# Gate rows gathered as high and low parts, overflow tables one chunk later, squares added in pairs on GpSimd, in a float32 decoder trunk

## The chip, the cores and the metric

One core of a Trainium2 chip runs the whole program. The metric is the device time of one execution in microseconds, the median over several runs. PE is the matmul engine (TensorE), DVE is VectorE, ACT ScalarE, POOL GpSimd, SP the engine that issues most transfers.

## The reference, cut to what matters

256 tokens of 1024 channels pass two layers of a token mixer and a channel mixer, all in float32.

```python
for layer in range(2):
    h = rms_norm(x, mix_norm[layer])
    x = x + hybrid_mixer(h, ...)
    h = rms_norm(x, ffn_norm[layer])
    x = x + (swiglu(h, ...) if layer == 0 else moe_ffn(h, ...))
return rms_norm(x, final_norm)

# in hybrid_mixer
a, b, p, gc, gp = split(h @ w_in)
u = a * sigmoid(b)
u = depthwise_conv(u, 31 taps, 512 channels) + bias     # causal
u = silu(layer_norm(u))                                  # over the 512 channels
merged = sigmoid(gc) * (u @ w_conv_out) + sigmoid(gp) * pooled(p) * pool_scale
return merged @ w_out

# in moe_ffn: 8 experts, each token goes to its best 2
y = sum_e comb[:, e] * (silu(t @ w_gate[e]) * (t @ w_up[e])) @ w_down[e]
```

## The kernel before, in words

Weights are streamed from HBM in units of 128 x 2048 numbers (1 MB), by SP, into a ring of places. For each unit ACT writes the high part (`w_hi`, line 674, a rounding to the one-pass matmul format) and DVE the low part (`w_lo`, line 1008, the difference). A product is then three one-pass matmuls, high by high, high by low, low by high (lines 1482 to 1484). A unit's place among the split places comes free when PE has used the unit (`unit_used`). Units are numbered within a mixer as U+0, U+1, ..., and within an item (one expert with the up to 128 tokens that go to it) from U0; "unit 11" of an item is U0+11. PE takes them in this order, and ACT and DVE go through them in it too, with their other work placed between splits by hand: `split_to(n)` brings an engine's splits up to unit n-1. The order of each engine's instructions is what the program text says; nothing is planned at run time.

**Mixer.** Each layer's mixer goes through 21 units. u is made by ACT (sigmoid, line 766) and DVE (`u_rows`, line 1125) in two halves, turned by PE (line 1561), copied by ACT. The convolution is 4 blocks of channels (c = 0 to 3) by 31 taps of 128x256: DVE does c = 0, c = 2 and the last taps of c = 3 (line 1057, with sums in PSUM); the other taps are products by ACT (line 709), added up by POOL (line 595). `SHARED` says how many taps of c = 3 go that way. DVE joins the two sums of c = 3 (line 1068). In the midst of slab U+12 PE runs `statistics` between the slab's two units: four plain float32 matmuls for the mean (line 1618), the matmuls of the pooling windows (lines 1572 to 1574), four for the variance (line 1624). A plain float32 matmul appears as two passes. Between mean and variance DVE subtracts the mean (line 1163), and ACT squares (line 815) into `sq`, half of the channels at a time. DVE goes on with splits up to U+15 behind the subtraction.

**Router and first item.** After the second mixer PE computes logits, ranks and totals; DVE makes tables of which token goes to which row of which item. An expert with more than 128 tokens gets an extra item; `overflow_tables` and `combination_table` serve those. The first item is started early: its gate products are computed for all 256 tokens at once (`gate_of_all_tokens`, units 0 and 1), and the rows of its tokens are then picked by a matmul with the 0/1 matrix `onehot`, in `gather_gate` (line 1814), which runs between units 2 and 3. Its source `gate_rows` is ACT's copy of the two PSUM banks (line 933). The token columns are picked in `gather_turned`; ACT and DVE split them (lines 904 and 1378).

**Items.** Items 0 to 7 have 7 chunks (c = 0 to 6) of 6 units each. In a chunk DVE multiplies silu of gate by up (line 1427), PE turns the result (line 1662) between the chunk's first and second gate units, ACT and DVE split it (lines 928 and 1402). In item 0's chunk c = 1 the gate units are 4 and 5, and the product of that chunk is followed by the tables and then by the splits of units 11 and 12. An item's result is added to `sums` in HBM by an indirect transfer in the item after it.

**End.** All but the last item's share is read back from `sums` into `xs` (line 491), the final norm of it made by ACT and DVE (from line 972 and line 1450), and rows of the last item are treated apart.

```python
            sp.wait_ge(scattered, n_items * 16)
            for b in range(TB):
                sp.dma_start(xs[:, b, :], sums[b * P:(b + 1) * P, :]).then_inc(sums_landed, 16)
```

Of the kernel before, what the change touches and what calls it, by code (L numbers as in the profile page):

```python
# [45 lines left out]
def trunk_kernel(nc, x, mix_norm, w_in, conv_dw, conv_dw_b, conv_ln_g, conv_ln_b, w_conv_out, w_pool, pool_scale,  # L46
# [19 lines left out]
    SHARED = 13  # L66
# [157 lines left out]
    with ExitStack() as ctx:  # L224
# [91 lines left out]
        gate_rows = tok_rows  # L316
# [45 lines left out]
        mean_done, centred, centred_sq, var_done = sem("mean_done"), sem("centred"), sem("centred_sq"), sem("var_done")  # L362
        std_ready, normed, silu_conv = sem("std_ready"), sem("normed"), sem("silu_conv")
# [6 lines left out]
        gate_copied, gate_gathered = sem("gate_copied"), sem("gate_gathered")  # L370
# [62 lines left out]
        def _(sp):  # L433
# [55 lines left out]
            sp.wait_ge(scattered, n_items * 16)  # L489
            for b in range(TB):  # L490
                sp.dma_start(xs[:, b, :], sums[b * P:(b + 1) * P, :]).then_inc(sums_landed, 16)
# [34 lines left out]
        def _(pool):  # L526
# [61 lines left out]
            for l in range(L):  # L588
# [8 lines left out]

                pool.wait_ge(gain_landed, seen.next(gain_landed, 16))
# [22 lines left out]
            def item(i):  # L621
# [23 lines left out]
                                    bounds_check=S - 1, oob_is_err=False).then_inc(last_base_landed, 16)  # L645
            seen.item = None
# [11 lines left out]
        def _(act):  # L658
# [18 lines left out]
            def rstd(b):  # L677

                return small[:, 6 + b:7 + b]
# [77 lines left out]
            def mixer(l, U, M):  # L757
# [51 lines left out]
                tap_products(l, 44)  # L809
# [122 lines left out]
            for b in range(TB):  # L932
                act.activation(gate_rows[:, b * N:(b + 1) * N], bank[R_LOW[b]][:, :], ACT.Copy, scale=rstd(b)).then_inc(gate_copied, 1)
# [55 lines left out]
        def _(dve):  # L989
# [123 lines left out]
            def mixer(l, U, M, x_left=None, x_right=None):  # L1113
# [27 lines left out]
                conv_taps(8)  # L1141
                split_to(U + 6)
                u_rows(1, M.high)
# [207 lines left out]
            def overflow_tables():  # L1351

                dve.wait_ge(total_done, 1)
                step(dve.tensor_scalar(over[:, 0, :], bank[TOTAL][:, 0:E], float(P), None, ALU.is_gt))
# [18 lines left out]
            overflow_tables()  # L1373
# [33 lines left out]
            def item(i):  # L1407
# [5 lines left out]
                for c in range(FC):  # L1413
# [14 lines left out]
                    if first and c == 1:  # L1428
                        combination_table()
                        dve.wait_ge(tables_ready, 1)  # L1430
                        shares(1, step).then_inc(onehot_ready, 1)
# [45 lines left out]
        def _(pe):  # L1477
# [120 lines left out]
            def mixer(l, U, M, x_right, next_left):  # L1598
# [13 lines left out]
                def statistics():  # L1612
                    for c in range(CC):
                        if c == 1:
                            pe.wait_ge(prod_added, len(ADDS) * l + last_add[c])
                        else:
                            pe.wait_ge(conv_step, CONV_STEPS * l + {0: TAPS + 1, 2: CONV_STEPS - 1, 3: CONV_STEPS}[c])
                        last = nc.tensor.matmul(bank[M.mean][:, 0:S], mean_w[:, :], conv[:, c, :], start=c == 0, stop=c == CC - 1)  # L1618
                    last.then_inc(mean_done, 1)
                    pool_windows(M.pooled)  # L1620
                    for c in range(CC):
                        if c % 2 == 0:
                            pe.wait_ge(centred_sq, seen.next(centred_sq))
                        last = nc.tensor.matmul(bank[M.var][:, 0:S], mean_w[:, :], sq[:, c * S:(c + 1) * S], start=c == 0, stop=c == CC - 1)  # L1624
                    last.then_inc(var_done, 1)
# [184 lines left out]
            def gather_gate():  # L1810

                for h in range(2):
                    for b in range(TB):
                        last = nc.tensor.matmul(low[0][:, h * S:(h + 1) * S], onehot[:, b, :].bitcast(F32),
                                                gate_rows[:, b * N + h * S:b * N + (h + 1) * S], start=b == 0, stop=b == TB - 1)
                last.then_inc(gate_gathered, 1)
# [18 lines left out]
            pe.wait_ge(gate_copied, TB)  # L1835
# [69 lines left out]
```

## Time and profile before

| what | us |
|---|---|
| median of 3 runs (1419.68 to 1420.81) | 1419.75 |
| the profiled execution's own time | 1420.94 |
| its span, first to last instruction | 1419.2 |
| PE busy in the span | 1405.4 |
| DVE busy | 1176.6 |
| ACT busy | 985.3 |
| POOL busy | 212.8 |
| last weight load issued (SP) | 1373.5 |
| last matmul ends | 1409.4 |
| first work on the rows read back from `sums` | 1403.7 |

The mean granted PE clock is 0.997 of full speed. The profiled execution is 1.2 us above the median; what is worked out from its rows is a difference, to be put on either. Times of day in the text (84.22, 489.07) are us from the start of the span.

### The profile page before, as it was taken

The page shows a single profiled execution, that of the slowest core. Times are in us where ns is not written, and L with a number is a line of the kernel's source. Part 1 is how long each engine was busy: PE and PEld are TensorE (multiplying, and loading weights), DVE is VectorE, ACT ScalarE, POOL GpSimd, SP SyncE. Part 2 cuts the span into 40 slices and gives each one's busy share as a digit, 9 for nine tenths or more (in the row PEclk, how much of TensorE's full clock was granted, in tenths as well). Part 3 has the DMA queues.
Part 4 walks back from the last instruction along what each step waited for, and adds up shares of the span by engine and source line. Part 5 has one row for each costly group of instructions (what it writes and reads, how often), then busy time and mean ns, then how long its engine had stood idle before and what let it go on. Part 6 is the DMA issues. An engine that isn't in the chain of part 4 may idle for free.

```text
span 1419.2 us, 18324 instructions
## 1 busy us (share of the span) xinstructions
PE 1405.4 (99%) x6490; PEld 1166.0 (82%) x6490; DVE 1176.6 (83%) x1069; ACT 985.3 (69%) x869; POOL 212.8 (15%) x251
## 2 busy tenths in 40 slices
PE   9999999999999999999999999999999999999997
PEld 7888888888888888888888888888888888888885
DVE  6997544548987998889899898888989889888896
ACT  7765434347765877867867777786786777778675
POOL 6840000005831101001001001000100100100020
PEclk9999999999999999999999999999999999999998
DMA  9656555545548899999999999999999999999992
GB/s 360 213 177 216 181 180 193 191 152 204 171 170 303 287 402 363 370 369 410 375 383 371 390 369 371 388 384 356 409 373 383 370 390 370 368 396 389 363 389 85
DMA packets 197840, 446.45 MB, mean 315 GB/s; under 512 B 8570, under 2 KB 20138, under 8 KB 197792
## 3 DMA queue, kind: packets, MB, share of 16 engines
q1 hardware_dynamic: 192496, 432.57, 80.8%
q0 software_dynamic: 2592, 8.87, 2.3%
q10 hardware_dynamic: 2704, 4.38, 0.9%
q8 instruction: 28, 0.46, 0.1%
q14 instruction: 20, 0.16, 0.0%
HBM read 438.49 MB, written 7.86 MB: 315 GB/s over the span
## 4 chain that ended last, share of the span: by engine, by line
PE 93%; DVE 4%; DMA 1%; ACT 1%; SPq 0%; issue 0%; POOL 0%; ACTq 0%; POOLq 0%
PE bank L1482 29%; PE bank L1484 29%; PE bank L1483 29%; PE bank L1662 2%; DVE bank L1057 2%; DVE w_lo L1008 2%; DMA raw<-in_w_in_dram 1%; PE bank L1540 1%; ACT w_hi L674 1%; PE bank L1829 0%; DMA out_dram<-tokA 0%; SPq L460 0%; PE bank L1624 0%; PE bank L1804 0%; PE bank L1618 0%
## 5 line engine op out<-in xcount | busy, mean ns | idle before, releaser
L1008 DVE TENSOR_TENSOR w_lo<-raw,w_hi 128x2048 fp32r<-128x2048 f32 x256 | 582.8, 2291 | 134.3 <-ACT w_hi L674 134.1
L674 ACT ACTIVATE w_hi<-raw 128x2048 fp32r<-128x2048 f32 x256 | 488.1, 1912 | 200.1 <-PE bank L1484 198.8
L1482 PE MATMUL bank<-w_hi,dT_hi 128*128 128x512 f32 (+1 forms) x756 | 296.3, 392 | 0.0
L1484 PE MATMUL bank<-w_hi,dT_lo 128*128 128x512 f32 (+1 forms) x756 | 293.2, 388 | 0.0
L1483 PE MATMUL bank<-w_lo,dT_hi 128*128 128x512 f32 (+1 forms) x756 | 292.6, 387 | 0.0
L1482 PE MATMUL bank<-w_hi,cT_hi 128*128 128x512 f32 x492 | 194.3, 395 | 0.0
L1484 PE MATMUL bank<-w_hi,cT_lo 128*128 128x512 f32 x492 | 191.7, 390 | 0.0
L1483 PE MATMUL bank<-w_lo,cT_hi 128*128 128x512 f32 x492 | 191.6, 389 | 0.0
L1484 PEld LDWEIGHTS bank<-w_hi,dT_lo 128*128 128x128 f32 x756 | 141.9, 188 | 29.4
L1482 PE MATMUL bank<-w_hi,hT_hi 128*128 128x512 f32 x416 | 164.1, 394 | 1.3 <-DVE hT_lo L1022 1.0
L1482 PEld LDWEIGHTS bank<-w_hi,dT_hi 128*128 128x128 f32 x756 | 142.0, 188 | 28.4
L1483 PEld LDWEIGHTS bank<-w_lo,dT_hi 128*128 128x128 f32 x756 | 142.1, 188 | 28.1
L1484 PE MATMUL bank<-w_hi,hT_lo 128*128 128x512 f32 x416 | 162.1, 390 | 0.0
L1483 PE MATMUL bank<-w_lo,hT_hi 128*128 128x512 f32 x416 | 162.0, 389 | 0.0
L615 POOL TENSOR_TENSOR small<-small 128x1 f32<-128x1 f32 x19 | 31.5, 1657 | 832.5 <-DVE next_rows L1331 458.5
L1008 DVE TENSOR_TENSOR hT_lo<-raw,hT_hi 128x2048 fp32r<-128x2048 f32 x57 | 130.5, 2289 | 10.5 <-ACT hT_hi L674 10.4
L674 ACT ACTIVATE hT_hi<-raw 128x2048 fp32r<-128x2048 f32 x57 | 109.1, 1915 | 20.8 <-PE bank L1484 20.8
L1484 PEld LDWEIGHTS bank<-w_hi,cT_lo 128*128 128x128 f32 x492 | 92.4, 188 | 19.6
L1482 PEld LDWEIGHTS bank<-w_hi,cT_hi 128*128 128x128 f32 x492 | 92.4, 188 | 18.2
L1483 PEld LDWEIGHTS bank<-w_lo,cT_hi 128*128 128x128 f32 x492 | 92.5, 188 | 18.2
L595 POOL TENSOR_TENSOR work<-work,tap_prod 128x256 f32<-128x256 f32 x80 | 91.3, 1142 | 11.8 <-POOL work L595 0.4
L1482 PEld LDWEIGHTS bank<-w_hi,hT_hi 128*128 128x128 f32 x416 | 78.1, 188 | 17.8 <-DVE hT_lo L1022 1.2
(260 smaller groups left out, 1859.0 us busy)
## 6 DMA issues: line engine op xcount, KB each, us to landing
raw<-in_moe_w_gate_dram SPq DMA_DIRECT2D x96, 1024.0 KB, 7.5
raw<-in_moe_w_up_dram SPq DMA_DIRECT2D x72, 1024.0 KB, 10.3
raw<-in_moe_w_down_dram SPq DMA_DIRECT2D x72, 1024.0 KB, 9.0
raw<-in_w_in_dram SPq DMA_DIRECT2D x20, 1024.0 KB, 5.7
mix<-in_moe_w_up_dram SPq DMA_DIRECT2D x16, 1024.0 KB, 8.5
gates<-in_moe_w_down_dram SPq DMA_DIRECT2D x16, 1024.0 KB, 11.2
gates<-in_moe_w_up_dram SPq DMA_DIRECT2D x16, 1024.0 KB, 8.7
work<-in_moe_w_down_dram SPq DMA_DIRECT2D x16, 1024.0 KB, 10.9
```

The lines of the kernel that those rows point to most:

```text
L595: pool.tensor_tensor(conv[:, c, :], part, tap_prod[:, (len(PRODUCTS) * l + n) % PRODS, :], ALU.add).then_inc(prod_added, 1)
L615: pool.tensor_tensor(small[:, 15:16], small[:, 14:15], small[:, 14:15], ALU.add).then_inc(gate_passed, 1)
L674: act.activation(w_hi[split_place(u, seen.item is not None)][:, 0:width], place[slot][:, 0:width], ACT.Copy).then_inc(hi_ready, 1)
L1008: dve.tensor_tensor(w_lo[split][:, 0:width], place[slot][:, 0:width], w_hi[split][:, 0:width].bitcast(F32), ALU.subtract).then_inc(lo_read ...
L1057: ins = dve.scalar_tensor_tensor(dst, src, tap, sum_, ALU.mult, ALU.add)
L1482: nc.tensor.matmul(dst, a_hi, b_hi, start=start, stop=False)
L1483: nc.tensor.matmul(dst, a_hi, b_lo, start=False, stop=False)
L1484: return nc.tensor.matmul(dst, a_lo, b_hi, start=False, stop=stop)
L1540: last = nc.tensor.transpose(bank[banks[k // 2]][:, (k % 2) * S + b * P:(k % 2) * S + (b + 1) * P], source[:, b, k * P:(k + 1) * P], ident ...
L1662: last = nc.tensor.transpose(bank[banks[b]][:, f * P:(f + 1) * P], tokP[:, b, f * P:(f + 1) * P], ident[:, :])
```

## The change

- `SHARED` goes from 13 to 14: one more tap of c = 3, in each layer, is a product by ACT and an add by POOL, one fewer a tap of DVE.
- In the first layer DVE does twelve taps and u's second half, and only then the split of unit U+5; in the second layer the order stays.
- POOL adds the squares of channel blocks 0 and 1, and of 2 and 3; PE's variance takes two matmuls instead of four. The adds stand ahead of POOL's scaling of the pool gates.
- The first item's gate rows are kept as a high part, written by ACT, and a low part, written by DVE, in the tiles `hT_hi` and `hT_lo`; the gather is four one-pass matmuls of 512 columns instead of four plain float32 ones of 256.
- The overflow tables, but for their first instruction, move from before the first item to its second chunk (c = 1), ahead of the combination table.
- The two transfers that read `sums` back are issued by POOL behind its last indirect read, not by SP behind the last weights.

```diff
-    SHARED = 13
+    SHARED = 14
...
-        gate_rows = tok_rows
+        gate_hi, gate_lo = (t[:, :, :].rearrange("p k s -> p (k s)")[:, 0:TB * N] for t in (hT_hi, hT_lo))
...
-            sp.wait_ge(scattered, n_items * 16)
-            for b in range(TB):
-                sp.dma_start(xs[:, b, :], sums[b * P:(b + 1) * P, :]).then_inc(sums_landed, 16)
...
+                for i in range(2):
+                    pool.wait_ge(centred_sq, seen.next(centred_sq))
+                    pair_of = sq[:, 2 * i * S:(2 * i + 1) * S]
+                    pool.tensor_tensor(pair_of, pair_of, sq[:, (2 * i + 1) * S:(2 * i + 2) * S], ALU.add).then_inc(sq_paired, 1)
+
                 pool.wait_ge(gain_landed, seen.next(gain_landed, 16))
...
                                     bounds_check=S - 1, oob_is_err=False).then_inc(last_base_landed, 16)
+            for b in range(TB):
+                pool.dma_start(xs[:, b, :], sums[b * P:(b + 1) * P, :]).then_inc(sums_landed, 16)
...
-                tap_products(l, 44)
+                tap_products(l, 45)
...
-                act.activation(gate_rows[:, b * N:(b + 1) * N], bank[R_LOW[b]][:, :], ACT.Copy, scale=rstd(b)).then_inc(gate_copied, 1)
+                act.activation(gate_hi[:, b * N:(b + 1) * N], bank[R_LOW[b]][:, :], ACT.Copy, scale=rstd(b)).then_inc(gate_hi_ready, 1)
...
-                conv_taps(8)
-                split_to(U + 6)
-                u_rows(1, M.high)
+                if l:
+                    conv_taps(8)
+                    split_to(U + 6)
+                    u_rows(1, M.high)
+                else:
+                    conv_taps(12)
+                    u_rows(1, M.high)
+                    split_to(U + 6)
...
-            overflow_tables()
+            dve.wait_ge(total_done, 1)
+            step(dve.tensor_scalar(over[:, 0, :], bank[TOTAL][:, 0:E], float(P), None, ALU.is_gt))
+            for b in range(TB):
+                part = slice(b * N, (b + 1) * N)
+                dve.wait_ge(gate_hi_ready, b + 1)
+                dve.scalar_tensor_tensor(gate_lo[:, part], bank[R_LOW[b]][:, :], rstd(b), gate_hi[:, part].bitcast(F32), ALU.mult,
+                                         ALU.subtract).then_inc(gate_lo_ready, 1)
...
                     if first and c == 1:
+                        overflow_tables()
                         combination_table()
...
-                    for c in range(CC):
-                        if c % 2 == 0:
-                            pe.wait_ge(centred_sq, seen.next(centred_sq))
-                        last = nc.tensor.matmul(bank[M.var][:, 0:S], mean_w[:, :], sq[:, c * S:(c + 1) * S], start=c == 0, stop=c == CC - 1)
+                    for c in (0, 2):
+                        pe.wait_ge(sq_paired, seen.next(sq_paired))
+                        last = nc.tensor.matmul(bank[M.var][:, 0:S], mean_w[:, :], sq[:, c * S:(c + 1) * S], start=c == 0, stop=c == 2)
...
-                for h in range(2):
-                    for b in range(TB):
-                        last = nc.tensor.matmul(low[0][:, h * S:(h + 1) * S], onehot[:, b, :].bitcast(F32),
-                                                gate_rows[:, b * N + h * S:b * N + (h + 1) * S], start=b == 0, stop=b == TB - 1)
+                pe.wait_ge(gate_lo_ready, TB)
+                for b in range(TB):
+                    for part in (gate_hi, gate_lo):
+                        last = nc.tensor.matmul(low[0], onehot[:, b, :], part[:, b * N:(b + 1) * N],
+                                                start=b == 0 and part is gate_hi, stop=b == TB - 1 and part is gate_lo)
```

## Rows read from the trace of the kernel before

**Rows 1.** The page: busy time of each engine, share of the span, instructions.
```profile
PE 1405.4 (99%) x6490; PEld 1166.0 (82%) x6490; DVE 1176.6 (83%) x1069; ACT 985.3 (69%) x869; POOL 212.8 (15%) x251
```

**Rows 2.** Who waited for whom, PE: us in total, times, longest; first of five.
```profile
PE bank L1670 <- POOL ident L538: 1.6, 1, 1.6
```

**Rows 3.** The chain of work that ended last: start us, us, what.
```profile
87.98 1.82 PE bank L1624 x8
...
396.98 1.82 PE bank L1624 x8
...
464.81 1.73 PE bank L1814 x8
...
488.79 0.44 PE bank L1662 x4
```

**Rows 4.** Timeline, first layer, second half of u: start us, us, engine, line.
```profile
32.61 2.76 DVE L1008 TENSOR_TENSOR w_lo<-raw,w_hi 128x2048 fp32r<-128x2048 f32 x1 [0.34 <-ACT w_hi L674]
...
33.68 0.81 ACT L766 ACTIVATE tokA<-bank,small 128x256 f32<-128x256 f32 x2
...
36.21 0.66 PE L1561 MATMUL bank<-ident,tokA 128*128 128x128 f32 x4 [0.80 <-DVE tokA L1125]
```

**Rows 5.** Timeline, first layer, mean to variance.
```profile
81.92 0.74 POOL L595 TENSOR_TENSOR work<-work,tap_prod 128x256 f32<-128x256 f32 x1
...
84.22 0.42 DVE L1068 TENSOR_TENSOR work<-bank,work 128x256 f32<-128x256 f32 x1
...
86.16 1.23 ACT L815 ACTIVATE work<-work 128x512 f32<-128x512 f32 x2 [1.00 <-DVE work L1163]
...
86.64 3.42 DVE L1008 TENSOR_TENSOR w_lo<-raw,w_hi 128x1024 fp32r<-128x1024 f32 x2
```

**Rows 6.** Timeline, second layer: the second split, and the variance.
```profile
396.77 2.28 DVE L1008 TENSOR_TENSOR w_lo<-raw,w_hi 128x2048 fp32r<-128x2048 f32 x1
...
396.83 1.97 PE L1624 MATMUL bank<-work,mean_w 128*128 128x256 f32 x8
```

**Rows 7.** POOL against DVE: all tap adds (ns min/median/max), then timeline rows.
```profile
L595 POOL TENSOR_TENSOR work<-work,tap_prod x80: 728/742/2834, 29.8 to 391.3; 128x256 f32<-128x256 f32 x80
...
33.36 2.59 POOL L595 TENSOR_TENSOR work<-work,tap_prod 128x256 f32<-128x256 f32 x1
...
638.79 4.50 DVE L1008 TENSOR_TENSOR w_lo<-raw,w_hi 128x2048 fp32r<-128x2048 f32 x2
...
638.94 2.19 POOL L615 TENSOR_TENSOR small<-small 128x1 f32<-128x1 f32 x1 [56.69 <-DVE next_rows L1331]
```

**Rows 8.** Timeline before the first item: first and last table operation, copies, splits.
```profile
458.06 0.23 DVE L1355 TENSOR_TENSOR tap_prod<-tap_prod 128x64 f32<-128x64 f32 x1
...
459.43 1.27 ACT L933 ACTIVATE gates<-bank,small 128x512 f32<-128x512 f32 x2 [6.39 <-issue]
...
460.61 0.17 DVE L1370 TENSOR_TENSOR slot_of<-tap_prod 128x6 f32<-128x6 f32 x1
...
461.33 2.16 DVE L1378 SCALAR_TENSOR_TENSOR dT_lo<-bank,vecs,dT_hi 128x128 fp32r<-128x128 f32 x8 [0.56 <-ACT dT_hi L904]
...
463.47 2.28 DVE L1008 TENSOR_TENSOR w_lo<-raw,w_hi 128x2048 fp32r<-128x2048 f32 x1
```

**Rows 9.** Timeline, DVE in the first item's second chunk.
```profile
483.94 0.68 DVE L1427 TENSOR_TENSOR tokP<-bank,tokA 128x512 f32<-128x512 f32 x1
...
485.94 4.49 DVE L1008 TENSOR_TENSOR w_lo<-raw,w_hi 128x2048 fp32r<-128x2048 f32 x2
```

**Rows 10.** Before the tail: timeline, DMA to landing, and a window's busy us and clock.
```profile
1359.68 2.73 POOL L644 DMA_INDIRECT gates<-sums,current_row  x1 [0.57 <-issue]
...
1398.10 1.92 ACT L674 ACTIVATE hT_hi<-work 128x2048 fp32r<-128x2048 f32 x1 [0.80 <-PE bank L1484]
...
xs<-sums SPq DMA_DIRECT2D x2, 512.0 KB, 12.6
...
1411.00:1412.00 1.00, 0.00 (x0) 0.00 (x0) 0.23 (x2) 0.00 (x0) 0.53 (x1) 0.71 0.62 223
```

More of the change, by code:

```diff
@@ L362, in trunk_kernel @@
         mean_done, centred, centred_sq, var_done = sem("mean_done"), sem("centred"), sem("centred_sq"), sem("var_done")
+        sq_paired = sem("sq_paired")
         std_ready, normed, silu_conv = sem("std_ready"), sem("normed"), sem("silu_conv")
@@ L369, in trunk_kernel @@
         rw_hi_ready, rw_ready, xn_hi_ready = sem("rw_hi_ready"), sem("rw_ready"), sem("xn_hi_ready")
-        gate_copied, gate_gathered = sem("gate_copied"), sem("gate_gathered")
+        gate_hi_ready, gate_lo_ready, gate_gathered = sem("gate_hi_ready"), sem("gate_lo_ready"), sem("gate_gathered")
         logits_done, diff_ready, probs_ready = sem("logits_done"), sem("diff_ready"), sem("probs_ready")
@@ L1351, in overflow_tables @@
             def overflow_tables():
-                dve.wait_ge(total_done, 1)
-                step(dve.tensor_scalar(over[:, 0, :], bank[TOTAL][:, 0:E], float(P), None, ALU.is_gt))
                 step(dve.tensor_tensor(over_sum[:, :, :], earlier[:, :, :], over[:, 0, :].unsqueeze(1).to_broadcast([P, E, E]), ALU.mult))
@@ L1834, in _ @@
             gather_turned()
-            pe.wait_ge(gate_copied, TB)
             first_index = seen.next(onehot_ready)
```

## The prediction

> **What bounds the kernel.** The page's busy line comes first: PE is busy for 1405.4 us of a span of 1419.2 [rows 1], so almost every microsecond by which PE is held up, or by which its work shrinks, is a microsecond of the span. Next the waits of PE: five, 3.9 us together, the longest of them 1.6 us at the start [rows 2]. So a change can win two things only: PE's own time in what it replaces, and the waits it removes. It loses wherever it makes PE wait, as nothing behind PE absorbs it. The chain of waits prices the PE groups touched, since it counts each matmul to the start of the next: 1.82 us for the eight passes (four plain float32 matmuls of 256 columns) of the variance in either layer, 1.73 us for the eight of the gate gather [rows 3]. The chain puts PE's pieces 0.15 us behind the starts of their records, as the same group at 396.98 and 396.83 shows [rows 3, 6]; I use the records' times. Last the timeline at each edit, for what is late next.
>
> **Part 1, u in the first layer, and one tap fewer on DVE.** The split of unit 5 stood ahead of u's second half on DVE: it began at 32.61, ran to 35.37, and PE waited 0.80 us at 36.21 for its transposes [rows 4]. Now four more taps (0.39 us each, 1.6) come in its place, then u's rows, which need ACT's sigmoids of 33.68 to 34.49 [rows 4]. The rows end near 35.1, ahead of the 35.41 at which PE would have come: the wait goes, 0.8 us. The split moved behind them ends near 37.8; PE needs it after 0.4 us of transposes and twelve products of 0.227, at 38.6, so no new wait. But PE only arrives sooner at the next place where it is short, the layer's mean: DVE works without pause up to the join at 84.22, on which PE waits [rows 5]. What moves that join is the tap that leaves DVE: 0.39 us. POOL has one more add: its last ended at 82.66 [rows 5], the next takes 0.74 and 0.14 between them, so 83.54, ahead of DVE's 83.83. ACT's extra product lies in front of idle time. So all of part 1 is worth 0.4 us at the first layer's mean. In the second PE does not wait there: nothing.
>
> **Part 2, the squares added in pairs on POOL.** It takes two of four variance matmuls from PE, 0.9 us in each layer, and puts two POOL adds between ACT's squares and PE. PE reaches the variance 1.7 us after ACT starts squaring. The adds' undisturbed price is the median of the tap adds, 742 ns, but the longest of the 80 took 2834 [rows 7]. What ended the long ones is seen by laying POOL's rows over DVE's: the add of 33.36 starts inside the split of 32.61 to 35.37 (both of its inputs in SBUF) and ends at 35.95, 0.58 us behind the split's end [rows 4, 7]. The split in its turn took 2.76 instead of 2.29, having started 0.13 us into an add. So the two exclude each other. A convolution tap, with one input in PSUM, stretches no add.
>
> In the first layer DVE centres and at once splits units 14 and 15, from 86.64 to 90.06; of the 3.42 us the second, of full width, is 2.28, so the first ends near 87.8. ACT's first of two squares (1.23 us from 86.16) is ready at 86.78 [rows 5]. The first add therefore starts inside a split. It gets in between the two: the tiny POOL operation of 638.94 ended at 641.13, 0.05 us behind the first of two splits that follow each other [rows 7]. In the new times (0.4 earlier): first split ends 87.46, add one ends 88.06, the second split loses 0.48 us to it and ends 90.13, and the second add, ready only when the split has the port, ends 0.60 later at 90.73. PE's last variance matmul follows, 0.06 + 0.43: 91.2. Before, PE was through at 87.83 + 1.82 = 89.6 [rows 3]. **Cost 1.6 us.** Second layer, the same chain without the 0.4: the second split would end at 396.77 + 2.28 = 399.05 [rows 6], with 0.48 at 399.53, the add at 400.13, PE at 400.62 instead of 396.83 + 1.82 = 398.65. **Cost 2.0 us.** Bounds for both layers: below, undisturbed adds (PE needs 0.87 us instead of 1.82 and does not wait: with part 1, 2.2 us won); above, both adds behind both splits, 0.3 us more each. I take the chain above, as the blocked add is a repeated row, and both orders at the port end near each other.
>
> The Trainium skill (SBUF — State Buffer, section Who interferes with whom) says that a VectorE instruction with two SBUF inputs contends with a GpSimd instruction that reads SBUF, whoever is first having the shared pair for the whole instruction. The rows agree on who waits, but the split waited 0.48 us for an add with 0.61 left. By the page the second split and the second add would be 0.13 us later in each layer, 0.26 in all.
>
> POOL's scaling of the pool gates moves behind these adds, from 82.6 to about 91, and is read only after PE's twelve-product groups of unit 13 and the pool projection; its waits queue nothing that is due.
>
> **Part 3, the first item's gate.** PE: four one-pass matmuls of 512 columns, 0.91 us at 0.227, instead of 1.73: 0.8 us. DVE gets two operations of 0.7 us or little more (the product of this size takes 0.68 [rows 9]) and loses those from 458.06 to 460.78, 2.72 us of overflow tables [rows 8]. The two wait for ACT's copies, which start at 459.43 behind its DMA issues and end at 460.1 and 460.7 [rows 8]; so they end near 461.5, and the low parts of the tokens, which began at 461.33, are 0.15 late. The split of unit 3, 463.47 to 465.75 [rows 8], then ends at 465.9. PE needed it at 464.66 + 1.73 = 466.4 [rows 3]; now it would at 465.6 and finds it at 466.0. Of the 0.8 us, 0.4 stay. The tables removed here lay beside ACT's work: removing them starts nothing earlier.
>
> **Part 4, the tables in the second chunk.** The same small operations, 2.72 us, now stand behind the product at 483.94 and ahead of the splits of units 11 and 12, which began at 485.94 [rows 9]. Unit 11, the first of the two, was ready at 488.2, and PE took it at 489.07, behind its four transposes [rows 3]: a cover of 0.8 us for 2.7. Now ready at 490.9; DVE may come up to 0.3 us sooner because PE is 0.4 ahead: 490.8. PE is **1.7 us later** than before, and that includes part 3. Unit 12 then follows in time: its split ends at 493.0, PE comes at 493.5. Bounds: if DVE gained all of 0.4 and the cover were 0.2 larger, 1.4; if nothing, 1.9; if it were wholly hidden, 0.4 won.
>
> **Part 5, rows of sums read back by POOL.** Its issue moves from SP behind the last weights to POOL behind the indirect transfer of 1359.68 + 2.73 [rows 10]. 1 MB more then goes ahead of the last weight units. The last of them is issued near 1373.5 and split at 1398.10; were it to take the read-back's 12.6 us and the whole added transfer (2.5 us at the 400 GB/s of this stretch) on top, 9 us would be left [rows 10]. The rows read back, landing within 12.6 us or twice that, are there before the tail. POOL's next task is in the tail. Zero either way; without this cover, each microsecond of landing past 1403.7 would count.
>
> **Sum.** 1.6 + 2.0 + 1.7 = 5.3 us. The profiled execution, span 1419.2 and time 1420.94, would become 1424.5 and 1426.2; it is 1.2 above the median of the runs. From the median, 1419.75 + 5.3 = 1425.0.
>
> **Rivals.** (a) POOL keeps the port for its second add. Then this is done at 88.75 and 398.15, PE ends the variance at 89.2 and 398.6, so -0.4 and 0, and with part 4 the sum is +1.3: 1421.1, not slower within what can be told. It is decided by whether the second add's read is asked for before the first's ends. For: nothing makes the second add wait on the first. Against: successive POOL operations follow each other, and a waiting split got in 0.13 us before an add's end. 12%. (b) The adds of 256 columns are not blocked here: 2.2 won and 1.7 lost, 1419.2; with part 4 hidden too 1417.2. Against it stand all adds that began in a split. 9%. (c) Part 4 hidden, by an order of work that I misread, part 2 as forecast: 3.6 - 0.4 = +3.2, 1423.0. 12%. (d) PE's clock falls in the new stalls, of 2.3 us each with a matmul ahead. The granted clock fell from 1.00 (2.4 GHz) to the lower level (1.2 GHz) between 1411 and 1412, about 2 us after PE's last matmul [rows 10]. If the lower level lasted 2 to 4 us behind each of two or three stalls, half of it lost, 2 to 4 us come on top: 1427 to 1429. Against it: PE was busy until just before each, and has work in them. 12%. (e) All of the waits absent and POOL's relief larger than one tap: under 1416.9. 4%.
>
> **Chances and range.** My forecast 50%, (a) 12, (b) 9, (c) 12, (d) 12, (e) 4, 1 for something else without effect. 0.2%, or 2.8 us, is what a measurement of this kernel can tell from no change. Slower: forecast, (c), (d), 74%; same: (a), (b) and the rest, 22%; faster 4%. Range 1420.8 to 1428.0: it takes in (a), (c) and half of (d), and leaves out (b), (e) and the rest of (d).
>
> **What would show it.** The wait at the first layer's second u transposes gone. In both layers two POOL adds between squares and variance, the first over 1 us and the second over 2, and PE waiting about 0.6 and 2.3 us for them. The gate gather as four matmuls in about 0.9 us, and a wait of some 0.3 behind it. PE waiting near 2 us for the low part of unit 11. Adds of 0.74 us there, or no wait at unit 11, or a granted clock below 1.00 before the tail would prove me wrong.

## The result, and the profile after

The changed kernel takes **1428.88 us** in the median of six runs (1427.1 to 1431.1), the kernel before 1419.78 beside it on the same chip: a ratio of 1.0061, with a 95% interval of 1.0048 to 1.0074. It is 9.1 us slower; 5.3 were forecast. The ratio goes with the means of the runs, which differ by 8.6 us, more than with the medians. The profiled execution took 1429.35 us, with a span of 1427.5 (8.3 more than before) and a mean granted clock of 0.996.

The page of the kernel after, the counterpart of [rows 1]:

```profile
PE 1408.9 (99%) x6478; PEld 1167.4 (82%) x6478; DVE 1178.5 (83%) x1069; ACT 987.2 (69%) x871; POOL 223.6 (16%) x259
```

PE is busy for 3.5 us *more*, though its work became less: eight passes fewer in the two variances, four fewer in the gate gather. A PE that does less and is busy for longer has run slower somewhere. POOL's 10.8 us more are the two additional taps, the four adds and the blocking behind splits. The waits of PE, against [rows 2] (us in total, times, longest):

```profile
PE bank L1638 <- POOL work L599: 5.1, 4, 2.0
PE bank L1497 <- DVE w_lo L1013: 1.8, 1, 1.8
PE bank L1684 <- POOL ident L536: 1.6, 1, 1.6
...
PE bank L1633 <- DVE work L1073: 0.4, 1, 0.4
```

New are the first line, the adds of the squares (5.1 us in four waits, two in each layer), and the second, the low part of unit 11. The wait for u's rows is gone. The variance of the first layer in the timeline of the kernel after (start us, us, engine, line; in brackets the idle time before and who ended it), against [rows 5]:

```profile
85.74 1.23 ACT L820 ACTIVATE work<-work 128x512 f32<-128x512 f32 x2 [1.57 <-DVE work L1173]
...
86.22 3.95 DVE L1013 TENSOR_TENSOR w_lo<-raw,w_hi 128x1024 fp32r<-128x1024 f32 x2
...
86.45 4.30 POOL L599 TENSOR_TENSOR work<-work 128x256 f32<-128x256 f32 x2 [2.75 <-ACT work L820]
...
88.08 0.70 PE L1638 MATMUL bank<-work,mean_w 128*128 128x256 f32 x2 [0.51 <-POOL work L599]
...
90.81 1.22 PE L1638 MATMUL bank<-work,mean_w 128*128 128x256 f32 x2 [2.03 <-POOL work L599]
```

The two adds take 4.30 us (1.57 and 2.77) where two undisturbed tap adds take 1.5. DVE's two splits take 3.95 where they took 3.42, and the whole lengthening is the second's (splits that started in this stretch, ns least, median, longest; the first, of half width, is the 1219):

```profile
L1013 DVE TENSOR_TENSOR w_lo<-raw,w_hi x2: 1219/2017/2815, 86.2 to 87.4; 128x1024 fp32r<-128x1024 f32 x1, 128x2048 fp32r<-128x2048 f32 x1
```

PE waits 0.51 us for the first add and 2.03 for the second, which ends at 90.76; 90.73 was forecast. The last line of the timeline holds what was not: the same two passes of a variance matmul took 0.70 us at 88.08 and 1.22 at 90.81. The windows of the kernel after (columns: us, busy us of PE, PEld, DVE, ACT, POOL with instructions, granted PE clock, DMA share, GB/s) say why:

```profile
88.00:90.00 2.00, 0.70 (x2) 0.30 (x2) 2.00 (x1) 1.49 (x2) 2.00 (x2) 1.00 0.68 168
90.00:91.00 1.00, 0.19 (x1) 0.19 (x2) 1.00 (x3) 0.00 (x0) 1.00 (x2) 0.84 1.05 397
91.00:92.00 1.00, 1.00 (x3) 0.82 (x4) 0.37 (x1) 0.00 (x0) 1.00 (x2) 0.50 1.11 365
...
93.00:94.00 1.00, 1.00 (x4) 0.71 (x4) 1.00 (x1) 0.84 (x1) 0.22 (x1) 0.50 1.07 416
94.00:95.00 1.00, 1.00 (x6) 0.81 (x5) 0.97 (x3) 0.00 (x0) 0.00 (x0) 0.95 0.73 283
404.00:405.00 1.00, 1.00 (x5) 0.84 (x5) 0.32 (x2) 0.73 (x2) 1.00 (x2) 0.86 1.05 391
405.00:406.00 1.00, 1.00 (x3) 0.74 (x3) 1.00 (x1) 1.00 (x1) 0.94 (x1) 0.50 1.03 391
...
407.00:408.00 1.00, 1.00 (x4) 0.81 (x3) 0.93 (x3) 0.73 (x2) 0.00 (x0) 0.50 0.29 109
408.00:409.00 1.00, 1.00 (x5) 0.78 (x5) 0.93 (x4) 1.00 (x3) 0.00 (x0) 0.94 0.00 0
```

The granted clock, the third number from the end, goes from 1.00 (2.4 GHz) to 0.50 (1.2 GHz) and back. In the first layer PE did 0.70 us of work in the two microseconds from 88 and 0.19 in the next one; toward 91 the clock fell to its lower level and came back at 94. If the clock changed once inside a window, the means give the moment (0.84 in 90 to 91 is 0.32 us at half, 0.95 in 94 to 95 is 0.10), and the low stretch is 0.32 + 3 + 0.10 = 3.4 us. In the second layer it lies from 404.7 to 408.1, the same length (0.28 + 3 + 0.12). PE works almost without pause there, at half its pace: the chain of the kernel after counts 0.43 us for a matmul of 512 columns, then 0.23.

```profile
93.74 0.43 PE bank L1498
...
94.43 0.23 PE bank L1497
```

Half of 3.4 us is lost behind each layer's waits: **1.7 us each, 3.4 in all.**

The first item, against [rows 8, 9]: the low half of the gate rows and the gather, then the second chunk, in the timeline of the kernel after.

```profile
467.36 1.41 DVE L1386 SCALAR_TENSOR_TENSOR hT_lo<-bank,small,hT_hi 128x512 fp32r<-128x512 f32 x2 [2.10 <-ACT hT_hi L938]
...
472.02 0.39 PE L1829 MATMUL bank<-hT_hi,onehot 128*128 128x512 f32 x1
...
472.70 0.39 PE L1829 MATMUL bank<-hT_lo,onehot 128*128 128x512 f32 x1
...
473.16 0.50 PE L1497 MATMUL bank<-w_hi,dT_hi 128*128 128x512 f32 x1
...
490.90 0.69 DVE L1441 TENSOR_TENSOR tokP<-bank,tokA 128x512 f32<-128x512 f32 x1
...
494.03 0.17 DVE L1378 TENSOR_TENSOR slot_of<-tap_prod 128x6 f32<-128x6 f32 x1
...
495.64 4.49 DVE L1013 TENSOR_TENSOR w_lo<-raw,w_hi 128x2048 fp32r<-128x2048 f32 x2
...
497.98 0.50 PE L1497 MATMUL bank<-w_hi,dT_hi 128*128 128x512 f32 x1 [1.79 <-DVE w_lo L1013]
```

The four matmuls begin 0.227 us apart, so the gather takes 0.91 us, and the next product begins 0.23 us later than PE could have begun it. In the second chunk the splits begin 4.74 us behind the product, 2.00 before; PE waits 1.79 us.

**Where the 9.1 us came in.** The same points of both traces, each after minus before: the mean of the second layer, 395.80 less 392.51, +3.3 (the first variance and its low clock, 1.6 + 1.7); the last product ahead of the token gather, 464.82 less 457.79, +7.0 (2.0 + 1.7 more); the token gather's start, 465.24 less 458.03, +7.2 (a gap of 0.2 us in front of it, which a1, a3, a7 and b4 have too and the other traces haven't); the product behind the gate gather, 473.16 less 466.18, +7.0; unit 11, 497.98 less 488.99, +9.0; PE's last matmul, 1418.22 less 1409.05, +9.2. So hardly anything (0.2 us) is gained or lost in the 920 us from unit 11 to the end. The span grew by only 8.3 because POOL's last write stood behind a landing transfer before and not after, worth 0.9 (the last section comes back to it).

### The profile page after: what moved, and what is told of

Read it like the earlier page. It is cut to its first block, busy times and chain, and to the rows that moved or that the text cites. A ratio compares the mean times of both kernels' runs of the same rounds, so it can differ in the third digit from the quotient of the medians.

```text
span 1427.5 us, 18310 instructions
## 1 busy us (share of the span) xinstructions
PE 1408.9 (99%) x6478; PEld 1167.4 (82%) x6478; DVE 1178.5 (83%) x1069; ACT 987.2 (69%) x871; POOL 223.6 (16%) x259
## 4 chain that ended last, share of the span: by engine, by line
PE 93%; POOL 3%; DVE 2%; ACT 1%; issue 1%; DMA 0%; ACTq 0%; POOLq 0%; DVEq 0%
PE bank L1497 30%; PE bank L1499 30%; PE bank L1498 29%; POOL work L593 2%; PE bank L1676 2%; DVE w_lo L1013 1%; PE bank L1555 1%; PE bank L1844 0%; POOL work L599 0%; ACT w_hi L679 0%; DMA work<-in_mix_norm_dram 0%; POOL tokA L614 0%; POOL tokP L614 0%; ACTq L901 0%; PE bank L1568 0%
## 5 line engine op out<-in xcount | busy, mean ns | idle before, releaser
L1499 PEld LDWEIGHTS bank<-w_hi,hT_lo 128*128 128x128 f32 x416 | 78.8, 189 | 16.8
```

Source lines behind the costliest of these rows:

```text
L1499: return nc.tensor.matmul(dst, a_lo, b_hi, start=False, stop=stop)
```

## The experiments

Each kernel is timed against the kernel before on its own chip; the ratio has its 95% interval. The first four start from the changed kernel.

### a1_no_pairs: no adds of squares

PE's variance has its four matmuls on ACT's squares again; everything else stays changed.

```diff
-                for i in range(2):
-                    pool.wait_ge(centred_sq, ...)
-                    pool.tensor_tensor(pair_of, pair_of, sq[...], ALU.add)
...
-                    for c in (0, 2):
-                        pe.wait_ge(sq_paired, seen.next(sq_paired))
+                    for c in range(CC):
+                        if c % 2 == 0:
+                            pe.wait_ge(centred_sq, seen.next(centred_sq))
```

> The changed kernel with the variance as before: four matmuls on ACT's squares, no adds on POOL. Theory (POOL adds shut out by DVE's splits cost PE 3.6 us in two waits, and each wait is followed by 3.4 us at half clock, worth 1.7 us): all of this goes, and what is left is +1.8 us at unit 11 of the first item and -0.4 us from the tap and u's rows, so 1421.2 us and a granted clock of 1.00 up to the tail. Rival (the loss lies elsewhere, the pairs cost only their two waits): the clock still falls and the time stays at 1424 to 1425 us.

Measured: 1421.46 (11 runs, 1421.09 to 1423.6) beside 1420.28, ratio 1.0012 [1.0002, 1.0021]. The clock stays at 1.00 through the place where it fell (windows of this kernel):

```profile
88.00:90.00 2.00, 2.00 (x10) 1.71 (x10) 2.00 (x2) 1.95 (x4) 0.00 (x0) 1.00 0.66 145
90.00:92.00 2.00, 2.00 (x10) 1.64 (x10) 2.00 (x3) 1.19 (x1) 0.00 (x0) 1.00 1.05 405
```

Of the 9.1 us, 7.9 hang on the adds (9.1 - 1.2; by the means 7.0, 8.6 - 1.6). Waits cost 3.6 of them, as forecast, so 4.3 came on top (3.4 by the means); the two low stretches of the profiled execution are worth 3.4. The wait for unit 11 (1.8 us) is still there. The time is the 1421.2 that was expected. Two of the eleven runs, 1423.14 and 1423.6, stand 1.7 and 2.1 us above the median, at a mean clock of 0.997.

### a2_splits_wait: DVE's splits behind both adds

```diff
+                dve.wait_ge(sq_paired, 2 * (l + 1))
                 split_to(U + 16)
```

> The changed kernel with one wait more: DVE starts its splits of units 14 and 15 only when POOL has added both pairs. Theory (a DVE split with two SBUF inputs shuts out a POOL add): both adds take 0.74 us, PE waits for POOL less than 0.2 us, the variance's relief of 0.9 us in each layer is kept, the clock does not fall: 1419.8 - 0.4 - 1.8 + 1.8 = 1419.4 us. Rival (the adds are slow by themselves, as an operation that starts cold on POOL or that writes in place): they stay at 1.6 and 2.8 us, PE waits over 2 us, 1428 us or more.

Measured: 1429.56 (5 runs, 1427.44 to 1432.49), ratio 1.0074 [1.006, 1.0088]. No gain at all; 1419.4 was expected. The timeline of this kernel shows that the port was indeed what stretched the adds, and who took it next:

```profile
86.21 1.41 POOL L599 TENSOR_TENSOR work<-work 128x256 f32<-128x256 f32 x2 [2.75 <-ACT work L820]
...
87.18 1.20 PE L1639 MATMUL bank<-work,mean_w 128*128 128x256 f32 x4
...
87.57 3.51 POOL L607 TENSOR_TENSOR gates<-gates,row_gain 128x512 f32<-128x512 f32 x2
87.66 5.58 DVE L1013 TENSOR_TENSOR w_lo<-raw,w_hi 128x1024 fp32r<-128x1024 f32 x2 [1.59 <-POOL work L599]
```

The adds take 0.7 us each and PE goes through the variance without a pause. But POOL's next operations, the scaling of the pool gates, now fall on the splits, which take 5.58 us instead of 3.42 and start 1.4 later. PE pays for that further on; the waits of the profiled execution (1427.44, the fastest of the five, without a fall of the clock; the others are at a mean clock of 0.995 to 0.997):

```profile
PE bank L1556 <- DVE gates L1212: 3.8, 2, 1.9
PE bank L1498 <- DVE w_lo L1013: 1.8, 1, 1.8
...
PE bank L1498 <- DVE dT_lo L1180: 1.5, 2, 0.7
PE bank L1498 <- DVE cT_lo L1190: 1.4, 2, 0.7
```

### a3_fill: small matmuls in front of PE's two waits

The waits stay as long; PE gets something to do in them, products of the identity that nothing reads.

```diff
+                    for c, n in ((0, 2), (2, 8)):
+                        for _ in range(n):
+                            nc.tensor.matmul(bank[M.high[1]][:, 0:P], ident[:, :], ident[:, :], start=True, stop=True)
                         pe.wait_ge(sq_paired, seen.next(sq_paired))
```

> The changed kernel with small matmuls, which compute nothing that is used, put into PE's two waits for POOL in each layer (two before the first, eight before the second, about 0.2 us each), so that PE works nearly all of the time in which it waited before. Theory (the half clock behind each wait comes from PE's idleness in it, and costs 1.7 us a time): the waits for POOL end at the same point, the granted clock stays at 1.00 up to the tail, 1428.9 - 3.4 = 1425.5 us, with less spread between runs. Rival (the clock falls for another reason at these places, or its fall costs next to nothing): the time stays at 1428.9 us.

Measured: 1427.04, ratio 1.0047 [1.0034, 1.0061]; the five runs are 1425.22, 1425.46, 1427.04, 1427.26 and 1427.3. In the profiled execution the adds are as long as in the changed kernel (ns least, median, longest):

```profile
L599 POOL TENSOR_TENSOR work<-work x4: 1574/2172/2777, 86.3 to 398.9; 128x256 f32<-128x256 f32 x4
```

PE's second variance matmul can start no earlier, but the clock stays up (windows of this kernel):

```profile
90.00:92.00 2.00, 1.75 (x10) 1.37 (x9) 1.31 (x3) 0.62 (x2) 2.00 (x3) 1.00 1.05 401
...
404.00:406.00 2.00, 2.00 (x10) 1.65 (x10) 1.97 (x3) 0.75 (x3) 0.12 (x1) 1.00 0.79 301
```

Its span is 1423.5, 4.0 below the changed kernel's; 3.4 is what two falls cost. The other engines and the transfers do the same work there as before, so this speaks for PE's idleness as what brings the falls. It is one trace, of the fastest of five runs, and a2 and a4 below show that nearly equal waits bring a fall in one execution and not in another. The runs as a whole say less: 6.8 us above the kernel before in the medians, 9.1 in the changed kernel, so 2.3 of the 3.4 expected. Three of the five are 1.6 to 2.1 us above the other two, the price of one fall, with a mean clock of 0.997; where they lost it no trace shows.

### a4_late_tables: a2 and the tables in chunk c = 5

```diff
+                dve.wait_ge(sq_paired, 2 * (l + 1))
...
                     if first and c == 1:
-                        overflow_tables()
...
+                    if first and c == 5:
+                        overflow_tables()
+                        overflow_combinations()
+                        dve.wait_ge(tables_ready, 1)
```

> As the kernel in which the splits wait for POOL's adds, and the overflow tables with the extra items' shares move on to the sixth chunk of the first item (c = 5), where DVE's splits end some 4 us ahead of PE. Theory: the wait at unit 11 goes and no other takes its place, the gate gather keeps its 0.4 us: 1419.4 - 1.8 - 0.4 = 1417.2 us. Rival (DVE has no room for 2.7 us in any chunk of an item): a wait of 1 to 2 us for a low part in the sixth or seventh chunk, 1418.5 to 1419.5 us.

The last step of the combination table, which needs the overflow tables, moves along with them.

Measured: 1429.05 (5 runs, 1427.52 to 1429.48), ratio 1.0062 [1.0048, 1.0076]; 1417.2 was expected. Unit 11's wait is gone, so the tables do fit into a later chunk. Yet the profiled execution has a span of 1427.2 where a2's has 1425.6, 1.8 us less in waits and 3.4 more in falls: here the clock fell in both layers, in a2's not once. But for unit 11 PE waits for the same things in both. Its longest wait in a layer is the one for the gated sum, with full work on both sides, 1.87 us up to 110.02 and 1.92 up to 423.81 here, 1.91 up to 110.08 in a2. The windows of this kernel:

```profile
109.00:110.00 1.00, 0.00 (x0) 0.00 (x0) 1.00 (x3) 0.00 (x0) 0.00 (x0) 1.00 0.77 215
110.00:111.00 1.00, 0.98 (x9) 0.98 (x10) 1.00 (x2) 0.29 (x2) 0.00 (x0) 0.98 1.03 399
111.00:112.00 1.00, 1.00 (x5) 0.81 (x4) 0.76 (x3) 0.92 (x4) 0.00 (x0) 0.50 0.97 377
...
114.00:115.00 1.00, 1.00 (x5) 0.82 (x4) 1.00 (x2) 1.00 (x1) 0.00 (x0) 0.81 0.00 0
```

and one of a2:

```profile
111.00:112.00 1.00, 1.00 (x7) 0.82 (x6) 0.75 (x3) 0.99 (x4) 0.00 (x0) 1.00 0.99 383
```

The fall came at 111.0, 0.9 us after PE was back at work, and lasted 0.04 + 3 + 0.38 = 3.4 us; in the second layer it came at 425.0 and lasted as long. So one wait of 1.9 us between full work can bring a fall, and the same wait need not.

### a5_scale_first and a6_scale_late: POOL's first scaling ahead of the adds

a5 is a2 with the first half of the pool gates scaled before the adds, so that nothing of POOL's falls on the splits. a6 is a5 with the tables as in a4.

```diff
                 for h in range(2):
                     ...                                   # scaling of half h
+                    if h:
+                        continue
+                    for i in range(2):
+                        pool.wait_ge(centred_sq, seen.next(centred_sq))
+                        ...                               # the add of pair i
```

> As the kernel whose splits wait for POOL's adds, and POOL scales the first half of the pool gates before the adds again, where it is idle for 2.7 us, not behind them. Theory (what ate the gain there was the scaling, which took the port from DVE at once and made its two splits 5.6 us long instead of 3.4, so that DVE was late at four later places of each mixer): splits 3.4 us, the waits of PE on DVE's low parts and gates in the mixers gone or under 0.3 us each; 1420.3 - 0.4 - 1.8 + 1.8 = 1419.9 us, up to 1421.6 where the clock falls after the wait at unit 11. Rival (the 1.4 us by which the splits start later is itself too much for DVE's cover): the waits on dT_lo, cT_lo and the merged gates stay above 1 us together in each layer, 1424 us or more.

> The same with the overflow tables in the sixth chunk. Theory: no wait at unit 11 either, 1420.3 - 0.4 - 1.8 - 0.4 = 1417.7 us, a granted clock of 1.00 up to the tail and the first version below the kernel before. Rival: as there, 1422 us or more.

Measured: a5 1423.64 (7 runs) beside 1420.48, ratio 1.0028 [1.0017, 1.0039], with 1419.9 to 1421.6 expected; a6 1421.55 (11 runs), ratio 1.0009 [0.9999, 1.0018], with 1417.7 expected. The rival came true: the later start of the splits is itself too much for DVE. The waits of a5:

```profile
PE bank L1557 <- DVE gates L1213: 3.3, 2, 1.7
PE bank L1499 <- DVE w_lo L1014: 1.8, 1, 1.8
```

Adds of 0.73 us, splits of 3.43 us in all, no fall of the clock, and PE is still 1.7 us late in each layer, one piece of work further on: at the gated sum, which DVE makes after its splits and its other work of the layer. DVE starts its splits 1.4 us later (87.61, not 86.22) and PE needs 0.9 us less, 2.3 together, of which 1.7 comes out as a wait. DVE's cover there, the time by which it can be late before PE waits, is the difference, an estimated 0.6 us. So even unblocked the adds lose more than the 0.9 us that they take from PE in each layer. a5 less a6 is 2.1 us, the price of the tables in the second chunk, whose wait is 1.8; and two of a5's seven runs, 1425.22 and 1425.65, stand 1.6 and 2.0 us above its median at a mean clock of 0.997, while none of a6's eleven does.

### a7_no_pairs_late: no adds, tables late

> The changed kernel without the adds on POOL (variance of four matmuls) and with the overflow tables in the sixth chunk of the first item. Theory (tables cost 1.8 us in the second chunk and nothing in the sixth): 1420.3 - 0.4 - 0.4 = 1419.5 us, no wait of PE on a low part in the first item but for some 0.3 us behind the gather. Rival (the gather's low part costs what the gather saves): 1419.9 us.

The edits are those of a1 and the table part of a4. Measured: 1419.47 (11 runs, 1418.95 to 1419.78) beside 1420.48, ratio 0.9995 [0.9986, 1.0004]. Expected was 1419.5. This is the best version that the runs led to, 1.0 us below the kernel before and not to be told from it. On the same chip a6, which has the late tables too and the unblocked adds besides, takes 2.1 us more.

### The parts alone

Five kernels start from the kernel before, each with one part of the change: b1 the adds of squares, b2 the tables in the second chunk, b3 the gate rows as high and low parts (the tables stay ahead of the item), b4 part 1, b5 the rows of sums read back by POOL. Their diffs are the pieces of the diff above, for b2

```diff
-            overflow_tables()
+            dve.wait_ge(total_done, 1)
+            step(dve.tensor_scalar(over[:, 0, :], bank[TOTAL][:, 0:E], float(P), None, ALU.is_gt))
...
                     if first and c == 1:
+                        overflow_tables()
```

> The kernel before with one edit: the squares added in pairs by POOL, two variance matmuls. Theory: the second add ends about 0.6 us behind DVE's second split in both layers, PE waits 0.5 and 2.0 us in each, loses 2.0 us net in each layer, and 1.7 us more behind each wait where the clock falls: 1420.5 + 4.0 = 1424.5 us in runs without a fall, 1427.9 us with two, the median between, nearer the upper. Rival (the loss of the whole change is no sum of its parts, and without the extra POOL add the pairs fit): 1422 us or less.

> The kernel before with one edit: the overflow tables, but for their first instruction, in the first item's second chunk. Theory (cover of 0.85 us for 2.7 us): PE waits 1.8 us for the low part of unit 11, the removal before the item gives nothing back, 1420.3 + 1.8 = 1422.1 us, and 1.7 more in runs in which the clock falls behind that wait. Rival (the wait at unit 11 comes from the gather's low parts ahead of it, not from the tables): less than 0.5 us of wait, 1420.5 us.

> The kernel before with one edit: the first item's gate rows as high and low parts and the gather as four one-pass matmuls of 512 columns; the overflow tables stay ahead, on DVE. Theory: tables, low parts of the gate and low parts of the tokens now follow each other on DVE, so that PE waits 0.7 us for the first of the tokens' low parts and some 0.9 us for the low part of unit 3, and the gather's 0.8 us is lost: 1420.5 + 0.2 = 1420.7 us. Rival (DVE has cover here): no new wait, 1420.5 - 0.8 = 1419.7 us.

> The kernel before with the first part alone: one more tap of each layer as product and POOL add, and u's second half ahead of the split of unit 5 in the first layer. Theory: the wait of 0.8 us at u's transposes goes, PE gains 0.4 us at the mean (DVE-bound), 1420.5 - 0.4 = 1420.1 us. Rival (POOL, with one add more, is now what the join waits for, as the changed kernel's row shows with 0.7 us): PE gains 0.1 to 0.3 us only, 1420.3 us.

> The kernel before with one edit: the rows of the sums are read back by POOL's queue, 13 us earlier, among the last weights. Theory: the last weight units land up to 2.5 us later and have over 9 us of cover, nothing waits: 1420.5 us, no wait of PE or ACT on a transfer in the last item. Rival (POOL's end of the program starts earlier or the weights come late): a change of more than 0.5 us either way, with a wait in the trace.

| kernel | median | before | difference | ratio, interval |
|---|---|---|---|---|
| b1_pairs_alone | 1427.30 | 1420.28 | +7.0 | 1.0053 [1.0039, 1.0066] |
| b2_tables_alone | 1422.67 | 1420.48 | +2.2 | 1.0014 [1.0005, 1.0023] |
| b3_gather_alone | 1420.32 | 1420.28 | 0.0 | 1.0000 [0.9991, 1.0009] |
| b4_part1_alone | 1419.41 | 1420.28 | -0.9 | 0.9994 [0.9985, 1.0003] |
| b5_sums_alone | 1420.07 | 1420.28 | -0.2 | 1.0000 [0.9991, 1.0009] |

The sum is +8.1, against 9.1 for the whole, which is no difference, since the intervals of the changed kernel and of b1 are each nearly 4 us wide. b1's trace repeats the pattern without any other part, the waits and then the low clock:

```profile
PE bank L1629 <- POOL work L602: 5.1, 4, 2.0
```

and b1's windows:

```profile
90.00:91.00 1.00, 0.00 (x0) 0.00 (x0) 1.00 (x3) 0.00 (x0) 1.00 (x2) 0.91 0.99 385
91.00:92.00 1.00, 0.92 (x3) 0.82 (x3) 0.65 (x2) 0.00 (x0) 1.00 (x2) 0.50 1.04 406
```

Its runs reach from 1425.84 (mean clock 0.997) to 1430.57 (0.993). b2 has the unit 11 wait, 1.8 us, and nothing else that is new. In b3 the low halves of the gate rows queue behind tables that are still there, start at 460.96 and push the low parts of the tokens to 462.29; PE waits 0.8 us for them, which is what the gather saves. So it was the removal of the tables from that place that let the gather gain anything, a coupling of parts 3 and 4. b4's trace has the earlier join (83.72) and, like the changed kernel's, no wait for a landing at the end (see the last section). b5 has no new wait of note; the two reads take 8.9 us from issue to landing in its trace and in that of the changed kernel, 12.6 before [rows 10].

## Why the prediction fell short

**The path, right.** Before, PE was the bound, and every term was a wait or a piece of PE's work. It held: point by point the difference grows only at the places named, and by only 0.2 us from unit 11 of the first item to PE's last matmul.

**Part 1, the size right, by luck.** The wait at u is gone. The gain at the first mean is 0.4: the join for which PE waits began at 84.22 [rows 5] and now at 83.81. But the forecast had the join wait for DVE's last tap (83.83) and POOL's additional add ready before it (83.54). The add was done at 83.70 and DVE's tap at 83.10, 0.7 us before the forecast, so that DVE stood idle for 0.71 us until POOL was through: DVE had won more than one tap, and POOL, 0.16 later than forecast, let only 0.4 of it pass. Two errors met in the same term. b4 measured -0.9 beside the -0.4 of this term; its interval holds both.

**Part 2, the waits right.** Forecast about 0.6 and 2.3, measured 0.51 and 2.03 in each layer, with the second add ending at 90.76 where 90.73 was worked out, and a cost of 1.6 and 2.0 us that the positions in the two traces repeat. Rival (a), POOL keeping the port, and rival (b), no blocking, are out: the adds of the changed kernel took 1.57 and 2.77 us, those of a2, with no split beside them, 0.7. The second split took 2.81 us, 0.53 longer than its 2.28, behind an add that by its record had 0.66 us left when the split began (87.36 to 88.02). In the row of the forecast it was 0.48 for 0.61. By the Trainium skill's rule (SBUF — State Buffer, section Who interferes with whom), that whoever is first has the shared pair for the whole instruction, the split would have waited for all that was left. Both records of this case fall 0.13 us short of that; the difference decided nothing.

**Parts 3, 4 and 5, right.** The gather takes 0.91 us, as forecast. Of the 0.8 us that it saves PE, 0.2 is left at the product behind it (+7.2 before, +7.0 there), where 0.4 was forecast. At unit 11 PE is 1.8 us later than at the token gather (+9.0 against +7.2), forecast 1.7 for parts 3 and 4 together; its wait there is 1.79, and 1.8 when alone in b2. Rival (c), tables hidden, is out. Part 5 nothing.

**The failed step** is the sum, which let every term of PE be at full clock and so put the price of a low clock behind the waits at nothing. The trace shows two low stretches of 3.4 us in its place, 3.4 us lost. It is rival (d), "PE's clock falls in the new stalls", with its 12%, that came true beside the forecast, at the two stalls of part 2: 5.3 + 3.4 = 8.7, against 9.1 measured and 9.2 at PE's last matmul. The reason given against it, that "PE was busy until just before each, and has work in them", does not hold. Laid out in time the two waits of a layer are one stretch, from 87.57 to 90.81, of which PE worked 0.7 of 3.2 us. And a4 shows that PE busy until just before is no safeguard: there a fall followed a single wait of 1.87 us between full work, where a2, with 1.91, had none. [Rows 10] had shown a fall about 2 us after PE's last matmul, which should have counted more than it did. At unit 11, a wait of 1.79 us, the clock stayed at 1.00, here as in the traces of a1, a5 and b2:

```profile
495.00:500.00 5.00, 3.21 (x17) 2.47 (x16) 4.90 (x6) 2.44 (x3) 0.00 (x0) 1.00 1.05 415
```

This is the window of the changed kernel that holds the wait. The price of rival (d), 2 to 4 us and 1427 to 1429, was right. So a stall's price was not its wait alone: the sum lacked a term that strikes in some executions, 1.7 us each time.

That it is the idleness and not the place rests on three things. b1 has the falls with nothing else changed. a3 has small work inside the same waits, no fall, and 4.0 us off the span. And in the 14 traces the clock is below 1.00 ahead of the tail in three only (the changed kernel, b1 and a4), twice in each, every time inside the layer's longest stretch of waiting or at most 1.3 us behind it, in a4 at another place of the layer than in the other two. What decides whether a given wait brings a fall stays open. How often it strikes varies: the six runs of the changed kernel are 1427.1 and 1427.2 at a mean clock of 0.997, 1428.7 to 1429.4 at 0.996, and 1431.1 at 0.993. Steps of about 1.7 us fit them, but only the profiled execution shows its falls; for the others that is argued.

**What remains open.** Some 0.4 us between 8.7 and 9.1 is in no term; the means differ by 8.6, so it is within the scatter. That the high runs of a1 and a5, 1.6 to 2.1 us above their medians, had a fall behind unit 11's wait fits a6 and a7, which lack the wait and have no such runs, but no trace shows it. The statement on part 2 that POOL's moved scaling "queue[s] nothing that is due" held in the changed kernel, but only since the adds were so late: in a2 the same scaling cost the splits 2.2 us.

## What to carry to other kernels

Before you hand work from the bounding engine to one that shares a port with a third, lay the third's timeline over the new operation: 0.9 us of PE work per layer was traded for 4.3 us of blocked adds, and freeing the port only moved the wait to the next work on DVE. Where a change makes PE wait, add up its idle time over the whole stretch, short pieces of work between waits included, and look for the granted clock in several traces near places where PE was that idle. The price is the wait and, in some of the executions, half of the low stretch behind it; one trace without a fall does not rule it out. Test a part against the slack of the engine that takes over (here 0.6 us on DVE behind the variance, 0.8 in the second chunk) before counting what it saves.

## What the runs showed of the hardware

- The low clock lasted 3.4 us each of the six times (two each in the changed kernel, b1 and a4), though PE was at work in nearly all of it. In the changed kernel's first layer it came at 90.7, at the end of 3.2 us in which PE had worked 0.7; in the second at 404.7, 1.2 us after the same pattern had ended at 403.51, with PE at work again. A single wait of 1.9 us brought it twice in a4 and not in a2; waits of 1.8 us (unit 11) and 1.7 us (a5, a6) did not in any trace.
- How long PE must stand idle before the clock falls is no fixed time in these traces. In the tail, where PE is idle for good, the fall comes between 1.9 us (b1) and 5.3 us (a6) after the end of the last matmul; the kernel before has 2.0, the changed kernel 3.3. The windows in which it fell, of b1, whose last matmul ends at 1416.67 (0.80 is 0.40 us at half, a fall at 1418.6), and of a6, where it ends at 1410.89 (a fall at 1416.2):

```profile
1418.00:1419.00 1.00, 0.00 (x0) 0.00 (x0) 0.45 (x3) 0.21 (x2) 0.30 (x1) 0.80 0.71 258
```

```profile
1416.00:1417.00 1.00, 0.00 (x0) 0.00 (x0) 0.00 (x0) 0.00 (x0) 0.47 (x1) 0.58 0.00 0
```

- A split of DVE that waits for the port gets it between two adds of POOL that are ready one behind the other (87.99), and an add that waits gets it between two splits (87.44). So here both engines took turns instruction by instruction, and it costs: 4.30 for two adds of 0.7, 3.95 for splits of 3.42.
- The end had 0.9 us in it that depends on a landing. The last write of POOL waited 2.69 us for the transfer of the output's first part before, 1.76 us for ACT's work alone after. The changed kernel's last write in the timeline:

```profile
1423.11 1.09 POOL L658 DMA_INDIRECT out_dram<-gates,current_row  x1 [1.76 <-ACT gates L990]
```

b4 and b1 did not wait for the transfer either (1.76 us); b2, b3 and b5 did, 2.72, 2.56 and 2.66 us, so none of parts 3, 4 and 5 alone removes it. Whether parts 1 and 2 do or the executions differ, one trace of each can't tell; it is 0.9 us of a span that none of the terms holds.
